# The first projection of all twelve own tiles in four blocks of 512 features, with float32 sums in SBUF

## What is computed

```python
mod = silu(c) @ w_ada + b_ada            # (B, 6*2048): shift and scale 1 and 2, gates
h = rms_norm(x, norm1_w) * (1 + sc1) + sh1
q, k, v, u, g = split(h @ w_in)          # 1024 columns each
att = diff_attention(q, k_all, v_all)    # 8 heads, after QK-norm and rotary
sgu = spatial_gating(u, g)
x = x + g1 * (concat(att, sgu) @ w_o)
x = x + g2 * (relu(modulate(x) @ w_ff1) ** 2 @ w_ff2)
```

## Time and profile before

| | us |
|---|---|
| median of 3 runs | 2465.95 |
| lowest and highest | 2463.79 to 2469.53 |
| span of the profiled execution, slowest core | 2459.1 |
| PE busy in it | 2356.5 |
| DVE busy | 1066.5 |
| ACT busy | 721.3 |
| POOL busy | 207.4 |

### The profile page before, as it was taken

The page is one execution under the profiler, slowest core; times in us unless marked ns, Lnnn a source line. Parts: engine busy times, 40 slices in busy tenths (PEclk is TensorE's granted clock), DMA queues, the critical chain, the costliest instruction groups (busy, mean ns, idle before and its releaser), DMA issues.

```text
span 2459.1 us, 38418 instructions; the slowest of 8 cores (2451.1 to 2459.1 us)
## 1 busy us (share of the span) xinstructions
PE 2356.5 (96%) x16224; PEld 1351.2 (55%) x16224; DVE 1066.5 (43%) x2129; ACT 721.3 (29%) x1185; POOL 207.4 (8%) x376
## 2 busy tenths in 40 slices
PE   2578999999999999999999999999999999999999
PEld 2367888787888854444444444444444444444444
DVE  2148763754732153553101332322524626528347
ACT  3056675765746561322231001001010010010110
POOL 2101121121100030000110000000000000000000
PEclk7679999999999999999999999999999999999999
DMA  9995786886625186966562222222433423323346
GB/s 208 171 218 156 110 118 94 110 115 111 101 50 83 32 135 140 255 202 129 87 108 52 52 52 52 52 52 52 90 65 64 90 52 75 80 50 81 64 94 188
DMA packets 168728, 251.56 MB, mean 102 GB/s; under 512 B 101104, under 2 KB 106864, under 8 KB 154480
## 3 DMA queue, kind: packets, MB, share of 16 engines
q0 software_dynamic: 54240, 164.94, 39.0%
q1 hardware_dynamic: 114320, 84.17, 13.9%
HBM read 348.28 MB, written 32.67 MB: 155 GB/s over the span
## 4 chain that ended last, share of the span: by engine, by line
PE 92%; DMA 5%; ACT 1%; another core or an unknown queue 1%; DVE 0%; POOL 0%; issue 0%; DVEq 0%; POOLq 0%
PE ps L454 92%; DMA ada<-wa 3%; DMA wr<-wa 1%; DMA xt<-xs 1%; ACT xn L487 0%; PE ps L464 0%; ACT hT L487 0%; POOL ada L575 0%; ACT P L487 0%; DVE xn L516 0%; DVE hT L516 0%; POOL wr L575 0%; ACT mod L487 0%; ACT st L497 0%
## 5 line engine op out<-in xcount | busy, mean ns | idle before, releaser
L454 PE MATMUL ps<-wf,aT 128*128 128x512 bf16 x3072 | 665.0, 379 | 0.0
L454 PE MATMUL ps<-hT,wf 128*128 128x512 bf16 x3072 | 665.0, 379 | 0.0
L454 PEld LDWEIGHTS ps<-hT,wf 128*128 128x128 bf16 x3072 | 300.4, 98 | 362.2 <-issue 0.8
L454 PEld LDWEIGHTS ps<-wf,aT 128*128 128x128 bf16 x3072 | 300.1, 98 | 362.5 <-issue 0.8
L487 ACT ACTIVATE tm<-ps 128x512 f32<-128x512 f32 x192 | 114.3, 597 | 1029.4 <-PE ps L454 1029.4
L454 PE MATMUL ps<-wr,hT 128*128 128x256 bf16 x3072 | 373.7, 277 | 6.9 <-DVE hT L516 4.6
L509 DVE TENSOR_TENSOR aT<-tm 128x512 bf16<-128x512 f32 x192 | 132.7, 692 | 548.8 <-ACT tm L487 546.0
L487 ACT ACTIVATE P<-ps 128x1024 bf16<-128x1024 f32 x304 | 295.8, 1020 | 128.9 <-PE ps L454 128.6
L454 PEld LDWEIGHTS ps<-wr,hT 128*128 128x128 bf16 x3072 | 297.3, 100 | 55.1 <-issue 18.5
L509 DVE TENSOR_TENSOR acc<-acc,ps 128x512 f32<-128x512 f32 x216 | 148.4, 687 | 157.5 <-PE ps L454 156.5
L454 PE MATMUL ps<-VV,P 128*128 128x129 bf16 x2432 | 164.1, 220 | 0.1
(11 more groups left out here) (144 smaller groups left out, 1460.7 us busy)
## 6 DMA issues: line engine op xcount, KB each, us to landing
wf<-wf POOLq DMA_DIRECT2D x64, 1024.0 KB, 8.5
wr<-wa POOLq DMA_DIRECT2D x96, 256.0 KB, 7.5
ada<-wa POOLq DMA_DIRECT2D x32, 512.0 KB, 44.0
xt<-xs POOLq DMA_DIRECT2D x14, 1024.0 KB, 8.2
wr<-wqkv POOLq DMA_DIRECT2D x48, 256.0 KB, 11.6
x1d<-xw SPq DMA_DIRECT2D x12, 1024.0 KB, 5.3
x1b<-x1d SPq DMA_DIRECT2D x48, 256.0 KB, 3.7
wo<-wo POOLq DMA_DIRECT2D x32, 256.0 KB, 15.7
```

Of the source, the lines that this page charges most:

```text
L454: ins = e.matmul(o, lhsT=l, rhs=r, start=st, stop=sp, skip_group_check=True)
```

## The change

The four blocks of the first projection now take in all twelve own tiles and four kinds: k, q and v of head pair 0 and v of head pair 1, 24 units in all. A unit's eight matmuls of a block form a closed sum in a bank; the sum is copied (block 0) or added (blocks 1 to 3) on DVE to a float32 tile `acc1` in SBUF, so banks are held only for a moment. The order inside blocks 1 to 3 is `VU` (all v) and then `KU` (k, then q). `kept_bank` does the sums; in block 3 a v unit goes from there to `VV`, a k or q unit to `chain_qk`, whose rotary part is the new `rope_in` (two instructions on POOL, a last scaling on DVE).

All own-tile loads, the modulation parts and the weights by blocks stand in one POOL queue in order of use (`plan`); x0 and x1 stay on SP. The modulation parts now have six buffers of one part each, x has four buffers for the own tiles, q's weights two slices. The 24 float32 tiles lie in the places of `hO`, of the own tiles' `xt` and `xn`, and of the `P` tiles. So the other tiles' loads, norms and transposes wait for sums that are drained (`staging`, `half_free`, `own_x`). Tiles 12 to 19 come in four groups of two; only k0, v0 and v1 remain to be projected for them. The k1 weights are loaded when k0's buffer is free, which is now near the end of `proj0`.

```diff
-    hO = S.sbuf("hO", [128, 16, 1024], BF16, SB + 62 * K)
+    hO = S.sbuf("hO", [128, 4, 16, 256], BF16, SB + 62 * K)
...
-    ada = [S.sbuf("ada%d" % i, [128, 16, 512], BF16, b) for i, b in enumerate((SB + 62 * K, SB + 78 * K, b0))]
-    adas = Pool(S, range(3))
-    xt = [S.sbuf("xt%d" % i, [128, D], F32, b) for i, b in enumerate((p1, p1 + 8 * K, slot1))]
-    xts = Pool(S, range(3))
-    xn = [S.sbuf("xn%d" % i, [128, D], BF16, slot1 + (8 + 4 * i) * K) for i in range(5)]
-    xns = Pool(S, range(5))
+    NPART = 6
+    ada = [S.sbuf("ada%d" % i, [128, 4, 512], BF16, b0 + i * 4 * K) for i in range(NPART)]
+    adas = Pool(S, range(NPART))
+    xt = [S.sbuf("xt%d" % i, [128, D], F32, b) for i, b in enumerate((SB + 86 * K, SB + 78 * K, slot1 + 17408, z1 + 4 * K, p1, p1 + 8 * K))]
+    xts = Pool(S, range(4))
+    xta, xtb, xtp = Pool(S), Pool(S), Pool(S)
+    xpool = [xts] * 12 + [xta, xtb, xta, xtb, xtb, xta, xta, xtp]
+    xn = [S.sbuf("xn%d" % i, [128, D], BF16, slot1 + i * 4 * K) for i in (2, 3, 0, 1)]
+    xns, xno = Pool(S, range(4)), Pool(S)
...
+    slices = [S.sbuf("wsl%d" % i, [128, 4, 256], BF16, b0 + 24 * K + i * 2048) for i in range(2)]
+    slcs = Pool(S, range(2))
+    OWN = range(0, 12, 2)
+    VU = [(1, "v", t) for t in (4, 6, 8, 10, 0, 2)] + [(0, "v", t) for t in OWN]
+    KU = [(0, "k", t) for t in (4, 6, 8, 10, 0, 2)] + [(0, "q", t) for t in (4, 6, 0, 2, 8, 10)]
+    where = {u: SB + (78 * K + i * 2048 if i < 4 else 62 * K + (i - 4) * 2048) for i, u in enumerate(VU)}
+    for i, u in enumerate(KU):
+        where[u] = p1 + i * 2048 if i < 8 else slot1 + (i - 8) * 2048
+    LATE = VU[:4] + KU[8:]
+    KN = KU
+    acc1 = {k: S.sbuf("ac_%d%s%d" % k, [128, 512], F32, b) for k, b in where.items()}
+    drained = {k: Ev() for k in where}
...
     def loads0():
         def ada_load(u):
-            j = yield adas
-            adabuf[u] = j
             for i in range(4):
-                c = slice(i * 2048, (i + 1) * 2048)
-                link(S.load(flat(ada[j])[:, c], wa0[u][:, c], "big%d_%d" % (j, i), cast=True), ada_ev[u][i])
-
-        def w_load(i):
-            link(S.load(flat(wring[i]), wqkv[i], "wr%d" % i, cast=True, parts=4), W0["qkv"[i]])
-        yield from ada_load(0)
+                j = yield adas
+                adabuf[u, i] = j
+                link(S.load(flat(ada[j]), wa0[u][:, i * 2048:(i + 1) * 2048], "ad%d" % j, cast=True), ada_ev[u][i])
+
+        def w_load(k, b):
+            c = slice(b * 1024, (b + 1) * 1024)
+            src = wqkv[3 * int(k[1]) + "qkv".index(k[0])][:, c]
+            if k != "q0":
+                i = ("k0", "v0", "v1").index(k)
+                W0s[k, b] = wring[i][:, 4 * b:4 * b + 4, :], None
+                link(S.load(flat(wring[i])[:, c], src, "wr%d_%d" % (i, b), cast=True), W0[k, b])
+            else:
+                j = yield slcs
+                W0s[k, b] = slices[j], j
+                link(S.load(flat(slices[j]), src, "wsl%d" % j, cast=True), W0[k, b])
         link(S.load(identb, ident, "ident", cast=True), ident_ev)
-        yield from ada_load(1)
-        w_load(0)
-        yield from ada_load(2)
-        w_load(1)
-        for u in range(3, 8):
-            yield from ada_load(u)
-        adabuf_ev.fire()
-        w_load(2)
-
-    adabuf = {}
-    adabuf_ev = Ev()
+        plan = ["x0", "x1", "a0", "x2", "x3", "a1", "v0", "k0", "q0", "x4", "x5", "x6", "x7", "v1", "x8", "x9", "x10", "x11"]
+        for b in range(4):
+            for it in plan if b == 0 else ["a%d" % (2 * b), "a%d" % (2 * b + 1), "v1", "v0", "k0", "q0"]:
+                if it[0] == "x":
+                    yield from x_load(int(it[1:]), xts)
+                elif it[0] == "a":
+                    yield from ada_load(int(it[1:]))
+                else:
+                    yield from w_load(it, b)
+        ada_out.fire()
+        for tt in range(12, 20):
+            yield from x_load(tt, xpool[tt])
+
+    def x_load(tt, pool):
+        j = yield pool
+        xbuf[tt] = j
+        q = tt >= 2
+        link(S.load(xt[j], xrows(tt), "x%s%d" % ("q" if q else "", j), cast=q), xev[tt])
 
...
+        yield xev[11]
+        ops = [S.load(qkw_t, qkw, "qkw"), S.load(lam_t, lamv, "lamv"), S.load(subw, sublnw, "subw"), S.load(sgw, sgunw, "sgw")]
         S.spawn(tables(ops), 28)
-        yield adabuf_ev
-        for tt in range(EARLY, 20):
-            yield from one(tt)
+        yield xnev[:12]
+        S.spawn(staging(), 12)
+        yield raw_ev
+        xno.give(0)
+        xno.give(1)
+        own_x.fire()
+
+    def staging():
+        xta.give(0)
+        yield [drained[k] for k in VU[:4]]
+        xtb.give(1)
+        yield [drained[k] for k in KU[:4]]
+        xtp.give(4)
+        yield [drained[k] for k in KU[4:8]]
+        xtp.give(5)
+        yield [drained[k] for k in KU[8:]]
+        xno.give(2)
+        xno.give(3)
+        yield xnev[12:20] + [group_ev[18]]
+        slot1_ev.fire()
...
-        j = yield xns
+        j = yield xns if tt < 12 else xno
...
-        xts.give(b)
+        if tt >= 12:
+            yield S.scale(xn[j], xt[b], st[:, 1:2])
+        else:
+            yield S.affine(xn[j], xt[b], st[:, 1:2], None)
+        xpool[tt].give(b)
         stats.give(st)
         xnbuf[tt] = j
...
-    def early_mod():
+    def early_mod(g):
         for b in range(4):
-            yield [mod_ev[b]] + raw_ev
-            ops = []
-            for t0, n, r in ((0, 4, 0), (4, EARLY - 4, 1)):
-                for kc in range(b * 4, b * 4 + 4):
-                    ops.append(S.affine(hts(kc, t0, n), hts(kc, t0, n), A1[:, kc, r:r + 1], S1[:, kc, r:r + 1]))
-            yield ops
-            h_ev[b].fire()
+            yield [mod_ev[b]] + raw_ev[4 * g:4 * g + 4]
+            r = 0 if g == 0 else 1
+            yield [S.affine(hts(kc, 4 * g, 4), hts(kc, 4 * g, 4), A1[:, kc, r:r + 1], S1[:, kc, r:r + 1]) for kc in range(b * 4, b * 4 + 4)]
+            h_ev[b][g].fire()
...
+        yield ho_free[(t0 - 12) // 2]
...
-        yield S.turn(dst[:, t0:t0 + 2].rearrange("p t h n -> p (t h) n"), kr[kj], "kr%d" % kj)
+        if p == 1:
+            yield slot1_ev
+        yield S.turn(dst[:, t0:t0 + 2].rearrange("p t h n -> p (t h) n"), zn, "kr%d" % kj)
         krs.give(kj)
...
+    def rope_in(z, kind, ti, rb, out, dead):
+        yield tab_ev
+        pool = (t1s, t2s)[ti // 2 % 2]
+        t2 = yield pool
+        ct, sn = (cosq, sinq) if kind == "q" else (cosk, sink)
+        d3 = ((256, 2), (64, 4), (1, 32))
+        yield [S.tt(bview(t2[:, hf * 32:hf * 32 + 1], d3), bview(z[:, 32 - hf * 32:33 - hf * 32], d3),
+                    bview(sn[:, ti, hf * 32:hf * 32 + 1], ((64, 2), (0, 4), (1, 32))), ALU.mult) for hf in range(2)]
+        z4 = bview(z, ((256, 2), (64, 4), (1, 64)))
+        yield S.tt(z4, z4, bview(ct[:, ti, :], ((64, 2), (0, 4), (1, 64))), ALU.mult, eng="pool")
+        yield S.tt(z, z, t2, ALU.add, eng="pool")
+        pool.give(t2)
+        yield S.tt(out.rearrange("p (g d) -> p g d", d=64), z.rearrange("p (g d) -> p g d", d=64), rb, ALU.mult)
+        dead.fire()
...
-    v0_end = Ev()
+    v_done = Ev()
+
+    def kept_bank(p, kind, t0, b, j, op):
+        key = (p, kind, t0)
+        a = acc1[key]
+        yield op
+        if b == 0:
+            yield S.copy(a, bank(j))
+            banks.give(j)
+        elif b < 3:
+            yield S.tt(a, a, bank(j), ALU.add)
+            banks.give(j)
+        elif kind != "v":
+            e = S.tt(a, a, bank(j), ALU.add)
+            e.then(lambda: banks.give(j))
+            chains[p].append(S.spawn(chain_qk(None, kind, t0, p, e), 18.5 + 0.1 * KU.index(key)))
+        else:
+            dst = VV[p][:, t0:t0 + 2, :, 0:128]
+            v4 = lambda x: x.rearrange("p (t h d) -> p t h d", t=2, h=2)
+            if t0 < 4:
+                vf = yield outs[p]
+                yield S.tt(vf, a, bank(j), ALU.add)
+                banks.give(j)
+                drained[key].fire()
+                yield S.copy(dst, v4(vf))
+                S.store(sv[t0 * 128:(t0 + 2) * 128, p * 256:(p + 1) * 256].rearrange("(t p) n -> p t n", p=128),
+                        vf.rearrange("p (t n) -> p t n", t=2), "sk").then(lambda: outs[p].give(vf))
+            else:
+                yield S.tt(dst, v4(a), v4(bank(j)), ALU.add)
+                banks.give(j)
+                drained[key].fire()
+            VVev[p][t0 // 2].fire()
 
     def proj0():
-        first = []
         for b in range(4):
-            yield [h_ev[b], W0["q"], W0["k"]]
             if b == 0:
-                for t0 in range(0, EARLY, 2):
-                    for k in range(2):
-                        j = yield banks
-                        first.append((j, k, t0))
-            for j, k, t0 in first:
-                op = S.mm([(bank(j)[:, i * 256:(i + 1) * 256], hts(kc, t0 + i), wring[k][:, kc, :], b == 0 and kc == 0 and i == 0, kc == 15)
-                           for i in range(2) for kc in range(b * 4, b * 4 + 4)])
-                if b == 3:
```

(54 more changed lines are left out.)

135 lines of the change are left out of this document (83 added, 52 removed).

## The result

| | before | after |
|---|---|---|
| median of 15 runs, us | 2466.05 | 2475.73 |
| ratio after / before | | 1.0033, 95% interval 1.0024 to 1.0042 |
| span of the profiled execution, slowest core | 2459.1 | 2472.4 |
| PE busy | 2356.5 | 2363.2 |
| block 3 starts, slowest core / mean of eight | 149.7 / 148.2 | 184.5 / 182.1 |

The change makes the kernel slower by 0.33%, 8 to 10 us, where 31 us less were predicted. (In some executions a whole die runs at a lower clock, before and after alike; those are left out of every ratio, and of the profile of e9_needed_first, which has such a die, only the other die is used.)

What follows compares the result with a forecast made beforehand. The load stream bounds until 144.82 us, then PE: 27.3 us ahead at block 3 plus 12.6 of old losses less L = 9 gives 31 off 2459.1, 2428; plus 6.85 makes 2435 us, range 2414 to 2458.

Steps and rivals of the forecast that it cites:

- 31 us: Whole kernel: predicted gain off the profiled span of 2459.1 us, summed as 27.3 + 12.6 - 9.
- What bounds the kernel: Up to the last modulation part at 144.82 us the load stream bounds; after that PE does.
- Block 3 comes later: Before block 3: 8 MB more in the stream at 3.15 us each delay its start from 149.7 to about 175 us.
- starved stream: Rival, chance 0.12: in the one load queue, busy x buffers stall modulation parts; 15 us lost, gain 16, 2450 us.
- 576 matmuls under the loads: Before block 3: 576 projection matmuls instead of 144, and 96 more transposes, hide 52.5 us of work; PE fits with 2 us spare.
- rival of the low clock: Blocks 1 to 3: PE stays at the low clock and falls behind, 46 us lost, 15 us slower, 2481; chance 0.08.
- The loss L: Block 3 to first scores: time beyond 70.0 us of PE work, taken as 9 us, between 2.6 and 24.
- cover for the last chains: Before the first scores: k1 and q1 run from 248 us while last k and q chains finish, keeping L near 9.
- DVE as the bound of the stretch: Rival, block 3 to first scores: DVE and ACT bound, 84 us of DVE against 70 of PE; L = 24, 2450; chance 0.13.
- Later stages at nothing: Attention after the first scores: k1, q1 and six ada1 columns fill PE in place of p1, costed at nothing.
- missing filler: Attention: if the next pair's projection does not fill PE, a few groups of scores idle 1.7 us each.
- The GpSimd rule: POOL's queue: two-SBUF-input DVE and SBUF-reading GpSimd instructions exclude each other; 16 POOL instructions might wait, 11 us, inside L's bounds.

Runs made afterwards that it cites:

- e9_needed_first: Changed kernel with k and q of tiles 0 to 3 first in the order of block units; ratio to the kernel before 0.9984.
- e7: Changed kernel reading only half of each modulation part of u = 2 to 7, 12 MB less; mean span 2433.1 us, one run.
- e5: Changed kernel with v1 put back behind the projection of head pair 0; ratio to the kernel before 1.0070.
- e4: Changed kernel with the sine table's work 12 us later in DVE's order; ratio to the kernel before 1.0037.
- e11: Changed kernel replanned with DMA latency 4.5 us for 1.9 and a higher price for POOL's scaling; ratio to the kernel before 0.9963.
- e1: Changed kernel with k1 and q1 weights, first ada1 weights and cached tiles held until the last Q transpose landed; ratio to the kernel before 1.0060.
- e15: Changed kernel replanned with 4.5 us DMA latency and dearer POOL scaling, k and q of tiles 0 to 3 first; ratio to the kernel before 0.9973.
- e13: Changed kernel replanned with only the planner's DMA latency raised from 1.9 to 4.5 us; ratio to the kernel before 0.9987.
- e6: Changed kernel without the loads of x tiles 14 to 19, working on old data; mean span 2476.7 us, one run.

## Why the prediction was wrong

I worked on the slowest core: 2428.1 was summed, 2472.4 measured, 44.3 us more. (The step from the span to the median, taken as 6.85 us, was 3.3, so the median is off by 41.) The miss lies in three places: block 3 at 184.5 in place of 175 (9.5 us), the stretch behind it at 105.0 in place of 79 (26.0), and the rest at 2182.9 in place of 2174.1 (8.8).

**What bounds the kernel: right in the main.** Up to block 3 the load stream counts (e7: 23.1 us back for 12 MB), but in the changed kernel PE's own work lies just as high, as the chain above shows. Behind block 3 it is PE, and what PE gets done under the loads comes off the end (e5: slower by 10.9 to 12.4 us without v1).

**Block 3 comes later by 8 MB x 3.15 = 25.2 us: direction right, size wrong.** It is 34.8 us on the slowest core and 33.9 in the mean, 9.6 and 8.7 more. Little of this lies in blocks 1 and 2: their 20 MB, priced at 63.0 us, take 63.27 us on the slowest core and 64.2 in the mean (117.9 to 182.1). The rest, 9.3 and 7.5 us, is there when block 1 starts. On the slowest core 8.75 us of it are the sine table's load in the chain, which the prediction has no line for. In the mean it is less: with that wait put off (e4) block 1 starts 3.6 us earlier and block 3 1.9 us, and the parts are then what comes last. A smaller piece is a thin place of the stream at 72 to 80 us: x8 to x11 are asked for one at a time as buffers come free, from 63.43 to 76.09, and the next modulation parts stand behind them in POOL's queue, at 76.61.

The stream itself has become a little slower. In e11 the mean from block 1 to block 3 is 65.5 us, 3.27 us per MB, and at a full share the DMA engines move 165 GB/s in 112 to 176 us in the changed kernel (below) and 167 in e11, where they moved 171 to 175 before on the eight cores in 50 to 100 us. Why was not tried. 0.12 us on each of the 50 MB ahead of block 3 would be 6 us, an estimate that carries the price of blocks 1 and 2 over to block 0; with the 25.2 that is 31.2, and e11 has 179.2 - 148.2 = 31.0. The window of block 0 and one of the blocks behind it, in the changed kernel:

```profile
72.00:80.00 8.00, 5.12 (x41) 3.87 (x40) 5.34 (x9) 5.59 (x11) 3.91 (x6) 0.71 0.72 244
112.00:176.00 64.00, 51.84 (x440) 40.50 (x440) 39.14 (x76) 7.85 (x12) 10.06 (x19) 0.87 1.05 165
```

That is the starved stream of the rivals, with 0.28 x 8 = 2.2 us of it against the 15 that I gave it. (The second row is at a share of 1.05, full.)

**576 matmuls under the loads: right.** Blocks 1 and 2 take 31.98 and 31.29 us on the slowest core (121.25, 153.23, 184.52), and most of their matmuls run at full clock (24 in 2.79 us, 0.116 us each with the time to fill; the first 48 of each block, behind a pause, took 7.76 and 7.07 us). PE did fit into 31.5 us, but not with the 2 us to spare that I summed, and by luck: I left out the 3.5 us a block in which PE waits for the modulation (0.79 and 2.71), and priced the parts at 0.62 and the `sel_t` matmuls at 1.84 us, where in blocks 1 and 2 they took 0.40 and 0.95 to 1.02, together 3.5 us less. The rival of the low clock, the one on the slower side, did not come true: the kernel is slower by another mechanism that was not on my list.

**The loss L = 9, bounds 2.6 to 24: wrong, and this is the step that failed.** On the slowest core it is 105.0 - 70 = 35. Of this 18.05 us are the wait for the Q transpose, 11.1 the other idle times of PE in the stretch (4.33 for POOL's scaling, 4.77 for a norm on ACT, 1.13, 0.54 and 0.31), and 75.9 - 70 = 5.9 matmuls and transposes at less than full clock (32 transposes in 3.56 us behind a wait, 1.95 without one). The last two together are 17 us, inside my bounds and 8 above the 9 that I took. The first has no line in the prediction at all. I wrote that the weights of k1 and q1 would be "asked for only when k0's buffer is free" and took them as cover for the last chains; I counted when these loads land, and not what else is on the DMA engines then. A transpose is a DMA too: of a step that is moved, the loads behind it move along, and what small transfers they meet has to be asked. In the kernel before, Q transposes took up to 14 us as well (median 8 on the slowest core), and the first scores waited for none of them; the first of them was asked for at 213.07 us there, 41 us ahead of the scores. That the loads are the cause is shown: e1, e9 and e11 take the wait away in three ways, by holding the loads, by the order of the units, and by the planner's latency; all three bring the first scores to 265 to 270 in the mean from 280.4 (e9: 270.3 on its four cores).

DVE as the bound of the stretch, the other half of L's upper end, did not come: DVE is busy 67.7 of 105.0 us, not 84.

**Later stages at nothing: wrong by 8.5 us** (8.8 with the rounding of the sum). Of it 5.0 is idle time (12.6 against 7.6), as much as the one row at 704.88, again a Q transpose; 3.5 is PE's busy time, 26.6 us less where 276 x 0.109 = 30.1 were due. The first matmuls behind each of the two waits are wholly or in part at the low clock (12 in 2.74 us, 28 in 5.14), 1.4 and 2.1 us more than at 0.109 each, which is that. I had looked for missing filler (1.7 us a group); no wait of this kind stands out in the changed kernel, and in e1, where k1 was held, the rest grew by 11.8 us, nearly all of it waits for K transposes.

**The GpSimd rule.** The Trainium skill (SBUF — State Buffer, "Who interferes with whom") was given 11 us along POOL's queue at most. POOL's rotary instructions, on float32 now, took 1.2 to 2.2 us where the earlier trace rows have 1.158 on bf16; some did take longer than others of their form, beside a DVE that was busy 64% of the time. No run separates this from anything else, and it stayed inside the 17 us.

**Where the 31 us are, then.** In the mean of the cores the change should have brought 31; e11, which is the same change with another order, has 7.0 (2455.1 to 2448.1), and the changed kernel -8.2. From the changed kernel to e11: 12.7 the wait, 2.4 the end of the projection (block 3 2.9 earlier). From e11 to the sum, 24 us: 5.8 in block 3 (179.2 against 148.2 + 25.2), of which 2.5 are blocks 1 and 2 (65.5 against 63.0) and the rest is there when block 1 starts; 9.3 in the stretch (86.1, where 102.7 - 25.9 = 76.8 was due), of which the waits for the norms of tiles 16 to 19 are the rows at 231.82 and 248.32; and 8.8 in the rest (2182.8 against 2174.0). Of that last figure a part can be read off: behind its first scores e11 has 9.5 us of waits, of which 4.3 are for ACT in the first groups of scores (267.16) and 3.5 for K transposes; e15 has the 4.3 too, but only 0.2 for K transposes, 6.0 in all, and its rest is 2178.3, 4.5 us shorter. So the collision is not gone in e11 either; a piece of it stands behind the first scores. The 4.3 us behind the rest of it are left open.

## What to carry to other kernels

When an edit moves matmuls under a load stream, list every DMA of the stretch behind it, the small ones too, and ask which of them is on the path while the buffers just set free are being filled: a transpose asked for ahead of 6 MB of weights landed in 2.4 us, one asked for among them in 20.5. The sine table is the same lesson a second time, 8.75 us on the slowest core. Here it was mended by issuing what is needed first ahead of the bulk (e9: 0.9984), not by holding the bulk back, which moved the wait (e1: 1.0060). A planner's latency is part of the kernel: with 4.5 us in place of 1.9 the same work ran 0.5% faster (e13). To judge the change apart from its plan, the kernel before would have to be planned with the same numbers, which no run here does. And when an experiment takes bytes or loads away under a planner, look at the order before you read its time: e6 and e7 both changed it.

## What the runs showed of the hardware

- On the slowest core a DMA transpose of q landed in 2.4 and 3.4 us with the DMA engines at a share of 0.41, and in 14.0, 20.5 and 18.5 us beside 3 x 1 MB of bf16 weights asked for between 265.0 and 274.4 us (share 1.05). With these loads held (e1) every one landed in 4.2 us or less. On cores that run the same program the wait for it was 4.4 to 18.05 us.
- A load of 256 KB on SP (the sine table) stood 7.2 to 9.0 us in the chains of five cores, beside a full stream.
- Scaling 128 x 2048 from float32 to bf16 took 5.44 us on POOL (one instruction), 1.5 on DVE in the mean of six (1.3 at the least) and 2.0 on ACT.
- The stream of cast loads at a full DMA share brought 171 to 175 GB/s before and 163 to 166 after on the eight cores; a block's MB took 3.15 us by the price of before, 3.21 in the changed kernel and 3.27 in e11. No run tells why.
- Behind a pause of PE of 18 us 12 matmuls took 2.74 us, 0.228 us each, against 0.109 us each at full clock; behind one of 5 us 28 took 5.14 us.
